# Issuing the stores of the MLP's activation blocks from GpSimd instead of SyncE and ScalarE

## What is computed

```python
def squared_relu_mlp(h, w_mlp_in, w_mlp_out):
    return jnp.square(jax.nn.relu(h @ w_mlp_in)) @ w_mlp_out

h = rmsnorm(x, g_pre_mlp[i]) * (1.0 + scale_f) + shift_f
y = squared_relu_mlp(h, w_mlp_in[i], w_mlp_out[i])
x = x + gate_f * rmsnorm(y, g_post_mlp[i])
```

## Time and profile before

| | us |
|---|---|
| median of 3 runs | 2146.02 (2144.93 to 2146.25) |
| the profiled execution | 2147.79 |
| its span | 2145.80 |
| first matrix, blocks 2 to 15 (subs 0 to 27) | about 936 to 1515 |
| PE busy from 960 to 1515, a stretch of 555 | 551.54 |
| DVE busy there | 506.00 |
| ACT busy there | 313.86 |
| POOL busy there | 0.00 |

### The profile page before, as it was taken

The page is one execution under the profiler, slowest core; times in us unless marked ns, Lnnn a source line. Parts: engine busy times, 40 slices in busy tenths (PEclk is TensorE's granted clock), DMA queues, the critical chain, the costliest instruction groups (busy, mean ns, idle before and its releaser), DMA issues.

```text
span 2145.8 us, 31955 instructions
## 1 busy us (share of the span) xinstructions
PE 2111.0 (98%) x11815; PEld 1814.5 (85%) x11815; DVE 1772.5 (83%) x1966; ACT 968.2 (45%) x1222; POOL 326.0 (15%) x198
## 2 busy tenths in 40 slices
PE   6999999999999999999999999999999999999998
PEld 4688888777777888889999999999888888888886
DVE  7987677678778635799989989989899898988988
ACT  5343434333344224455555555555634443444453
POOL 1000000000000001000000000000055463554634
PEclk9999999999999999999999999999999999999999
DMA  9976656664554442457767777775565566476664
GB/s 361 356 238 221 214 173 220 204 192 151 156 165 160 137 177 79 171 162 241 232 219 237 230 221 223 239 236 162 185 227 182 191 235 221 152 252 239 235 228 165
DMA packets 324766, 444.75 MB, mean 207 GB/s; under 512 B 20301, under 2 KB 184465, under 8 KB 319001
## 3 DMA queue, kind: packets, MB, share of 16 engines
q1 hardware_dynamic: 320642, 419.02, 59.2%
q10 hardware_dynamic: 3992, 23.93, 2.9%
HBM read 383.10 MB, written 59.79 MB: 206 GB/s over the span
## 4 chain that ended last, share of the span: by engine, by line
PE 84%; DVE 5%; DMA 4%; issue 3%; ACT 1%; DVEq 1%; SPq 1%; POOL 0%; POOLq 0%; ACTq 0%
PE pair L979 27%; PE pair L981 26%; PE pair L980 26%; DMA gf_item<-in_w_ada 2%; DMA am_item<-in_w_ada 1%; PE pair L1202 1%; DVE sw_lo L2828 1%; PE pair L1086 1%; PE pair L1060 1%; SPq L758 0%; DVE t_raw L2764 0%; DVEq L2732 0%; PE pair L1077 0%; DMA w_raw<-in_w_in 0%; PE pair L1126 0%
## 5 line engine op out<-in xcount | busy, mean ns | idle before, releaser
L979 PE MATMUL pair<-v_op,hid_r 128*128 128x512 f32 x896 | 348.9, 389 | 1.4 <-issue 1.1
L981 PE MATMUL pair<-v_op,hid_r 128*128 128x512 f32 x896 | 348.6, 389 | 0.0
L980 PE MATMUL pair<-v_op,hid_r 128*128 128x512 f32 x896 | 348.6, 389 | 0.0
L2932 DVE TENSOR_TENSOR v_op<-v_raw,v_op 128x1024 fp32r<-128x1024 f32 x192 | 295.6, 1561 | 55.8 <-ACT v_op L2072 54.8
L979 PE MATMUL pair<-in_hi,w_hi 128*128 128x512 f32 (+1 forms) x832 | 340.3, 409 | 0.0
L2072 ACT ACTIVATE v_op<-v_raw 128x1024 fp32r<-128x1024 f32 x192 | 203.2, 1060 | 275.1 <-PE pair L981 268.0
L981 PE MATMUL pair<-in_hi,w_lo 128*128 128x512 f32 (+1 forms) x832 | 322.3, 387 | 0.0
L980 PE MATMUL pair<-in_lo,w_hi 128*128 128x512 f32 (+1 forms) x832 | 321.2, 386 | 0.0
L1937 ACT ACTIVATE sw_hi<-sw_raw 128x1024 fp32r<-128x1024 f32 x196 | 207.4, 1058 | 214.7 <-PE pair L981 146.5
L3187 POOL TENSOR_TENSOR v_sum<-v_raw,v_raw 128x512 f32<-128x512 f32 x60 | 149.2, 2514 | 950.1 <-DVE v_raw L2947 950.1
L979 PE MATMUL pair<-in_hi,sw_hi 128*128 128x256 f32 x896 | 254.0, 283 | 2.7 <-DVE pair L2835 1.9
(11 more groups left out here) (326 smaller groups left out, 4097.7 us busy)
## 6 DMA issues: line engine op xcount, KB each, us to landing
v_raw<-in_w_mlp_out SPq DMA_DIRECT2D x128, 512.0 KB, 5.2
sw_raw<-in_w_mlp_in SPq DMA_DIRECT2D x112, 512.0 KB, 5.5
hid_r<-hid_scratch SPq DMA_DIRECT2D x112, 512.0 KB, 6.4
am_item<-in_w_ada SPq DMA_DIRECT2D x64, 512.0 KB, 8.3
af_item<-in_w_ada SPq DMA_DIRECT2D x64, 512.0 KB, 4.8
w_raw<-in_w_in SPq DMA_DIRECT2D x96, 256.0 KB, 3.4
w_raw<-in_w_in SPq DMA_DIRECT2D x160, 128.0 KB, 3.3
ag_item<-in_w_ada SPq DMA_DIRECT2D x32, 512.0 KB, 4.7
```

What stands on the lines that cost most here:

```text
L979: pe.matmul(dst, a[0], b[0], start=start, stop=False, skip_group_check=onto)
L980: pe.matmul(dst, a[0], b[1], start=False, stop=False, skip_group_check=onto)
L981: return pe.matmul(dst, a[1], b[0], start=False, stop=stop, skip_group_check=onto)
L2932: dve.tensor_tensor(v_op[i % 4][:, 1, :], raw_of(u, p)[:, h, :], v_op[i % 4][:, 0, :].bitcast(F32), ALU.subtract).then_inc(v_lo, 1)
```

## The change

All 56 stores of the pieces are issued by POOL, in the order block 0 pieces 0, 1, 2, 3, block 1 pieces 0, 1, 2, 3, and so on, each after a wait for the part that it stores. SP's `store_hidden` calls and ACT's `store_high` are gone. All four pieces count on `hid_out`, and `hid_low_out` is gone: ACT's wait ahead of the ReLU is now for all four pieces of the block before, as is DVE's.

```diff
-            for piece in range(4):
-                store_hidden(0, piece)
...
-                if stored:
-                    store_hidden(b - 1, 1)
...
-                if stored:
-                    store_hidden(b - 1, 3)
...
-            sp.wait_ge(hid_out, 48 * (FBS - 2))
-            sp.wait_ge(hid_low_out, HID_LOW_OUT_0 + 16 * (FBS - 2))
+            sp.wait_ge(hid_out, 64 * (FBS - 2))
...
-                    act.wait_ge(hid_out, 48 * b)
+                    act.wait_ge(hid_out, 64 * b)
...
-            def store_high(b, part):
-                rows = (slice(0, 3), slice(3, 7))[part]
-                act.wait_ge(h_hi, 2 * b + part + 1)
-                act.dma_start(hid_dram[b, :, rows, :], hid_r[0][:, rows, :].bitcast(F32)).then_inc(hid_out, 16)
-
             def relu_pair(b, n):
                 act.wait_ge(sw_used, STEPS * 2 * (b - NB + 1))
                 act.wait_ge(c22_ready, 2 * (b - NB + 1))
-                act.wait_ge(hid_out, 48 * b)
+                act.wait_ge(hid_out, 64 * b)
...
-                    if m == 1 and b - 1 < FBS - 2 and i in (F_P1, F_P2):
-                        store_high(b - 1, i // F_P2)
...
-                    dve.wait_ge(hid_low_out, HID_LOW_OUT_0 + 16 * b)
+                    dve.wait_ge(hid_out, 64 * b)
...
+            def store_hidden(b, piece):
+                rows = (slice(0, 3), slice(7, 10), slice(3, 7), slice(10, 14))[piece]
+                pool.wait_ge((h_hi, h_lo)[piece % 2], 2 * b + piece // 2 + 1)
+                pool.dma_start(hid_dram[b, :, rows, :], hid_r[0][:, rows, :].bitcast(F32))\
+                    .then_inc(hid_out, 16)
+
+            for b in range(FBS - 2):
+                for piece in range(4):
+                    store_hidden(b, piece)
             pool.wait_ge(gf_col, GF_COL_0 + 4)
```

More of the change, by code:

```diff
@@ L592, in build_block @@
         xs_raw, XS_RAW_0 = x_rstd, TB
-        hid_low_out, HID_LOW_OUT_0 = x_ss, TB
         xs_hi, XS_HI_0 = xt_act, KT
@@ L682, in load_m1 @@
                     .then_inc(w_in_s[mm % 2], 16)
[L684 to L688, removed]
             def load_quarter(u, role):
@@ L870, in _ @@
                 b, following = block_of(u), u + 1 < SUBS
-                stored = u % 2 and b - 1 < FBS - 2
                 sp.wait_ge(sw_lo_done, step_end(u, F_P7))
```

## The result

| | before | changed |
|---|---|---|
| median of 20 runs each, on the same chip | 2145.43 us | 2149.27 us |
| ratio, 95% interval | | 1.0018 [1.0011, 1.0024] |
| the profiled execution | 2147.79 us | 2150.11 us |
| its span | 2145.80 us | 2148.2 us |

The change costs (1.0018 − 1) × 2145.43 = **3.9 us**, with an interval from 2.4 to 5.1. The loss is small, but it is one. One of the 20 runs of the changed kernel took 2613.83 us, at a mean granted clock of 0.754 where all others have 0.998 or 0.999; it counts in the median, but not in the ratio.

What follows compares the result with a forecast made beforehand. PE was taken as the bound, idle only 4.30 us in the region touched. Gains 0 (at most 4.3), new wait 0 and POOL 0 left the time unchanged, forecast at the runs' median, 2146.0 us; range 2142 to 2151.

Steps and rivals of the forecast that it cites:

- the forecast case: Whole kernel: gains, new wait and POOL all 0, so 2146.0 us; own range 2142 to 2150; chance 0.81.
- the part on POOL: POOL takes 56 issues while otherwise idle; piece 3 lands after 5.3 us; order and place of pieces 1 and 2 cost nothing.
- the loads start no earlier than now: SP's queue in odd subs: weight loads behind stores have later waits of their own; gain 0, at most 0.84 us.
- Rival C: SP's DMA queue: loads gain without piece 3's store ahead, DVE's `gf_item` waits shrink; 2141.7 us; chance of over 0.2% 0.03.
- All four signs: 960 to 1515 us: PE busy near 551.5, ReLU without store wait, DVE operations 1.21 to 1.23, POOL's 1024 KB stores 5 to 7.
- SP's and ACT's relief: Freeing SP of 30 issues (10.2 us) and ACT of 26 (8.5 us) gains 0, at most PE's 4.3 us idle.
- Piece 3: POOL's store of piece 3 lands after 5.3 us, 4.6 for the transfer plus 0.7 for POOL; block 9's margin is 7.14.
- The new wait: ACT's ReLU of the next block also waits for piece 3: cost 0, landed 1.8 us ahead even in block 9.
- Rival A: ACT's ReLU in 13 even subs: piece 3 lands late, past 10.6 us; 2164 us at 12; chance 0.07.
- Rival B: 960 to 1515 us: POOL's 52 issues slow DVE by 1.1 us each, +8 to +33, 2166 us; chance 0.05.
- Rival D: Program start or end: POOL's DMAs cost 5 us for queue setup or a last wait, 2151 us; chance 0.04.
- the 1.9 us behind a PSUM sum of DVE: PE's 4.30 us idle in the changed region was said to lie mostly behind this sum, 1.9 us in 3 waits.

Runs made afterwards that it cites:

- piece 1, or piece 2, last: Changed kernel with POOL's order 0, 2, 3, 1 (piece 1 last): 2156.78 us, ratio 1.0058; with 0, 1, 3, 2 (piece 2 last): 2164.80 us, ratio 1.0093.
- block 0: Against the changed kernel, only block 0's four stores come from POOL, blocks 1 to 13 from SP and ACT as before: 2145.39 us, ratio 0.9999.
- POOL 1 and 3: Against the changed kernel, POOL issues pieces 1 and 3 and all of block 0, ACT pieces 0 and 2, SP none: 2145.89 us, ratio 1.0002.
- order 0, 2, 1, 3: Changed kernel with POOL issuing each block's pieces in the order 0, 2, 1, 3 instead of 0, 1, 2, 3: 2146.29 us, ratio 1.0007.
- POOL 0 and 2: Against the changed kernel, POOL issues pieces 0 and 2 of blocks 1 to 13, SP pieces 1 and 3 and block 0: 2146.24 us, ratio 1.0003.
- the old waits: Changed kernel with the waits of before: ReLU waits for pieces 0, 1, 2 alone, DVE's first combination for piece 3 alone: 2149.91 us, ratio 1.0019.
- all from SP: Kernel before with ACT's two stores moved to SP, at the place of piece 1; nothing on POOL: 2150.79 us, ratio 1.0030.
- stores twice: Changed kernel with every store issued a second time from POOL, into a second scratch tensor that nobody reads: 2217.95 us, ratio 1.0340.

## Why the prediction was wrong, point by point

**The time.** Forecast 2146.0, measured 2149.27: inside the range of 2142 to 2151, but the forecast case was no change, to within 0.2%, and the ratio lies at 1.0018, with most of its interval below that bound and its upper end above it. A small loss stood only in the upper end of that case, "0.3 us lost in each of 13 blocks, by transfers that fall otherwise"; measured are 2.97 / 13 = 0.23 us in each odd sub. That the size fits is luck, since no load was named there and none was looked at; in the sum the term stood at 0.

**The step that failed** is in the part on POOL: "Pieces 1 and 2 become ready within a microsecond of each other, as now ... so their order and place cost nothing". It asked only who waits for these two stores, and the answer, the ReLU some 15 us later, is right. It didn't ask whose transfer they stand beside, nor see that piece 2, ready 0.8 us ahead of piece 1, now stands behind the wait for piece 1. Piece 2 left 3.8 us ahead of A21 (1139.58 − 1135.82) and now leaves 2.2 us ahead of it; A21 landed 1.1 us later on average, and had had 1.0 us to spare on average, 0.3 in the tightest sub. Measured term: +2.97 us in the 13 odd subs, against 0 in the sum. Swapping two numbers in the order took it away.

**A second step** was half right: "the loads start no earlier than now". They do start at the same place: A21 7.33 us after the sub's first load in both. But an unchanged start was taken for an unchanged landing. Rival C had the sentence that was needed, "stores from a queue of their own take the same DMA engines", and used it only against a gain.

How far A21 may slip is read best across all kernels. The growth of an odd sub is its mean length less that of before, 20.19 us:

| kernel | A21 lands after, mean | growth of an odd sub |
|---|---|---|
| piece 1, or piece 2, last | 4.05, 4.09 | −0.05 us |
| before; block 0; POOL 1 and 3; order 0, 2, 1, 3; POOL 0 and 2 | 5.27 to 5.50 | 0.00 to +0.02 us |
| changed, three times (one with the old waits) | 6.32 to 6.37 | +0.20 to +0.23 us |
| all from SP | 6.96 | +0.73 us |
| stores twice | 10.98 | +4.7 us |

Up to 5.5 us it is free; from about 6.2 us on, each microsecond costs one: 6.96 − 0.73 = 6.2, 10.98 − 4.74 = 6.2. That is where it should be, since in the five kernels without a loss DVE comes to the sum 6.28 us after A21's issue on average (5.83 to 6.5). The last row holds some time at the lower clock too, and its exact fit is not to be leaned on. The changed kernel stands just past the edge. The three profiles of it take 534.02 us on average over the 26 subs, the five with no loss 530.18: 3.8 us, as much as the medians differ. Of this 2.75 us lie in the odd subs. The other 1.1 lie in even subs, which scatter between 265.8 and 269.5 in the five; so this part is not shown.

**What held.** All four signs that the prediction gave for being right came true, or nearly (PE busy 550.44 us, no wait of the ReLU for a store, DVE's splits at 1.22 us, POOL's 1024 KB landing after 5.2 to 6.7 us, two of them after 7.3), and none of them looks at a load; the loss of 3.9 us fits beside them. *SP's and ACT's relief brings nothing:* no kernel was faster. *Piece 3:* 5.3 us was taken, and that it fits is luck too: its 0.7 us for POOL is the length of a small addition, which has nothing in it of a DMA. In block 9 the low part ended at 1308.23 + 2.28 = 1310.51, POOL's issue began 0.29 us later and the store landed 5.4 us after that; the ReLU came 7.32 us after the low part's end, right behind the split ahead of it:

```profile
1308.23 2.28 DVE L2720 TENSOR_TENSOR hid_r<-hid_f,hid_r 128x2048 fp32r<-128x2048 f32 x1
...
1310.80 0.53 POOL L3156 DMA_DIRECT2D hid_scratch<-hid_r  x1 [7.38 <-DVE hid_r L2720]
...
1316.86 1.06 ACT L1917 ACTIVATE sw_hi<-sw_raw 128x1024 fp32r<-128x1024 f32 x1 [1.33 <-DVE sw_raw L2790]
1317.83 1.01 ACT L1859 ACTIVATE hid_f<-pair 128x1024 f32<-128x1024 f32 x1
```

Over the 13 blocks piece 3 was down 5.5 to 6.8 us after the low part, and the ReLU came after 7.3 to 8.2. *The new wait is free:* shown from both sides, by pieces 1 and 3 on POOL without a loss, and by the loss without the new wait. *Rival A* needed over 10.1 us and never came near. *Rival B, POOL slows DVE:* not so. The splits of the whole stage beside 52 issues of POOL, to be held against the earlier trace rows:

```profile
L2806 DVE TENSOR_TENSOR sw_lo<-sw_raw,sw_hi x196: 1211/1219/1227, 945.8 to 1515.2; 128x1024 fp32r<-128x1024 f32 x196
```

1219 ns against 1218. Here the row that was missing now exists, and it agrees with what the prediction took from the Trainium skill, page "SBUF — State Buffer", section "Who interferes with whom": descriptor generation leaves a two-input DVE operation alone. The other rule taken from that page, a POOL DMA starved by DVE, isn't tested here. The stores of piece 3 landed after 5.2 to 6.5 us while DVE was busy 91% of the time, but its operations there have two inputs, and the rule is about 2-port modes, of which no row tells.

*Rival C* has nothing for it: DVE's waits for `gf_item` are 29.7 and 30.1 us in two profiles of the changed kernel, against 21.2 to 28.2 in the five without the loss. *Rival D* is ended by the kernel with block 0 alone. One reading was loose: the 1.9 us behind a PSUM sum of DVE are less than half of PE's 4.30 us, not most of them.

## What to carry to other kernels

Where a DMA is moved to another queue, list not only who waits for it, but every load in flight beside it, and measure for each of those how long before its first use it lands: here one had 0.3 to 1.8 us, another (`gf_item`) nothing at all. On one queue issue first what is ready first; a wait in program order for a later piece delays bytes that could already be gone. And before bytes are moved out of one load's way, look at whose way they come into: the two kernels that freed A21 lost 11 and 19 us at the next load.

## What the runs showed of the hardware

- **The order within a queue changes when others land.** From one queue, piece 1 ahead of piece 2, these landed after 4.0 and 6.7 us, the last byte 4.5 us after A21's issue, and A21 after 6.4 on average. From one queue in the other order they landed after 5.8 and 4.5, the last byte 3.1 us after A21's issue, and A21 after 5.5. From two queues, with piece 2 first, they landed after 6.4 and 5.4, the last byte 3.5 us after A21's issue, and A21 after 5.3. So most of it is the order, and little the number of queues. The Trainium skill, page "DMA: Bandwidth & Descriptors", section "Issuing engines are not separate DMA queues", says that DMAs of all issuing engines run on the same 16 DMA engines and interleave, and that using several issuers saves only the time to issue. The rows agree with the first half as far as they go: a store from POOL holds up a load from SP. To the second they add a case: on one queue a ready store stands behind the wait for another, and that cost 3.9 us, while the order 0, 2, 1, 3, with the same time to issue, costs at most 3.4 and perhaps nothing.
- **The price of POOL as an issuer:** an issue takes 533 ns instead of 326 to 338, begins 0.3 us after its release instead of 0.03, and a 1 MB store alone lands after 5.3 to 5.4 us instead of 4.6. That is about 1 us per store, and it was hidden throughout. It is no fixed price: in the two kernels in which POOL issued another store 0.53 us behind piece 3, this landed after 4.4 us in most blocks. Why is not shown.
